# Splitting the mixed tokens at the entry of an MLP: two remainders earlier on VectorE, two on GpSimd

## The chip, the cores and the metric

One core of a Trainium2 chip. The time is the device time of one launch in microseconds, as the median of the runs shown. TensorE (PE in the profile) multiplies matrices, VectorE (DVE) and GpSimd (POOL) do elementwise work, ScalarE (ACT) activations and copies, SyncE (SP) issues DMAs.

## What is computed

A decoder step of two layers on 544 tokens (512 of a prompt, 32 of decoding requests) of width 1024: a token mixer and memory attention, and behind each an MLP of width 4096. The MLP is what matters here:

```python
x = x + jnp.concatenate([mix, mem_out], axis=-1) @ p['w_out'][l]
h2 = rmsnorm(x, p['norm2'][l])
x = x + jnp.square(jax.nn.relu(h2 @ p['w_mlp1'][l])) @ p['w_mlp2'][l]
```

## The kernel before

All data is float32. A product of precision near float32 is made of three passes of TensorE over operands split in two: a high part (a copy in the format that TensorE reads, made by ScalarE) and a remainder (operand less high part, a subtraction of two SBUF operands, made by VectorE or GpSimd). Tokens stand in columns, 544 of them in two halves of 272, features on 128 partitions in eight blocks k; KQ is 4.

The up projection of an MLP has 32 blocks of 128 output features. The first four (PLAIN) are made by `up_plain(j)`: eight blocks k times three passes times two halves, 48 matmuls each. From the fifth on two blocks form a pair, which `up_pair(n)` makes out of seven products q = 0 to 6 in place of eight. The products q = 2, 3 and 6 use mixed tokens: sums and differences of the token halves, three of 272 columns for each kk = 0 to 3, held in `mixed_tokens` (high parts at index 0, remainders at index 1). They come about thus, for each kk: VectorE mixes (`mix_tokens`, L1440: three instructions L1445, L1446, L1447 of 272 columns), ScalarE takes the high part of all three (`mixed_high`, L1063, the instruction L1066, 816 columns, semaphore `tok_hi`), and then VectorE takes the remainder (`mixed_token_rest`, L1449, the instruction L1452, 816 columns, semaphore `tok_lo`). TensorE waits for `tok_lo` only in the product q = 2 of the first pair (n = FIRST_DOWN).

Each engine works off its own list in program order, and the lists are held together by semaphores. Around the entry of an MLP they read so.

VectorE: the output projection's last block k = 7 (`out_units`), in which kk = 0 and 1 have been mixed at k = 5 and 6; `rest(u0 + KT - 1 + HL)`, a weight remainder (L1413, 1024 columns); mixing of kk = 2 and 3; a weight remainder; `inverse(r)` (L1433 and the reciprocal L1434, of 544 columns), which waits for ScalarE's root; a weight remainder; then for j = 0 to 3 `plain(j)`: a ReLU times the inverse root out of PSUM (L1537, semaphore `unit_out`), at j = 1 the four remainders of mixed tokens, and remainders of the first pair's weights (`up_rest`, L1503, 512 columns): q = 0 after j = 1, q = 1 and 2 after j = 2, q = 3 and 4 ahead of the ReLU of j = 3, q = 5 and 6 after it. The ReLU of j = 2 waits for the first hidden remainder of GpSimd, that of j = 3 for the second.

ScalarE: high parts of mixed tokens 1, then a weight's, of 2 and 3, the root (L1044), a weight's; then for each j the square of the ReLU (L1106, L1107) and high parts of the pair's weights (L1089): q = 0 behind j = 0, q = 1 and 2 behind j = 1, q = 3 and 4 behind j = 2, q = 5 and 6 behind j = 3; then the high part of a down weight (L1102) and the copy L1127 of product 0 from PSUM (semaphore `up_copied`), for which TensorE waits ahead of product q = 4.

GpSimd: the sum of squares (L1985); then in turn the hidden remainder of j = 0 (L2023), weight sums L2001 and L2007 (for q = 1 and 2), the hidden remainder of j = 1, the difference L2010 (for q = 3), the hidden remainder of j = 2, the difference L2014 (for q = 5), the hidden remainder of j = 3. ScalarE's high parts of q = 1, 2, 3 and 5 wait for these.

Of the kernel before, what the change touches and what calls it, by code (L numbers as in the profile page):

```python
# [52 lines left out]
KQ = KT // 2  # L53
# [81 lines left out]
def build(nc, xT, memT, hist, params, consts, ropes, weights, memK, memV, cacheK, cacheV, pages,  # L135
          o_y, o_pool, o_memk, o_memv, o_k, o_v, o_pools, o_vs):
    F32, F32R, I32 = mybir.dt.float32, mybir.dt.float32r, mybir.dt.int32
    ALU, ACT, AX = mybir.AluOpType, mybir.ActivationFunctionType, mybir.AxisListType

    ctx = ExitStack()  # L140
    with ctx:
# [13 lines left out]
        def place(name, shape, dt, at):  # L155
            return nc.alloc_sbuf_tensor_at(name, shape, dt, offset=at)
# [48 lines left out]
        mixed_tokens = place("mixed_tokens", [P, 3, 2, KQ, HALF], F32R, kv_at)  # L205
        mixed_raw = place("mixed_tokens_raw", [P, 3, 2, KQ, HALF], F32, kv_at)
# [44 lines left out]
        def sem(name):  # L251
            return ctx.enter_context(nc.semaphore(name))
# [39 lines left out]
        tok_raw, tok_hi, tok_lo = sem("tok_raw"), sem("tok_hi"), sem("tok_lo")  # L292
# [28 lines left out]
        def halves(ap):  # L321

            return ap.rearrange("p (a b) -> p a b", a=2)
# [47 lines left out]
        def hidden_tile(n, c):  # L371

            return 4 * (n // 2 % 2) + 2 * (n % 2) + c
# [1032 lines left out]
        def _(dve):  # L1406
# [33 lines left out]
            def mix_tokens(l, kk):  # L1440

                dve.wait_ge(tok_raw, KT * l + KQ + kk + 1)
                at = Z[:, KQ + kk, :]
                t2, t3, t4 = (mixed_raw[:, c, 1, kk, :] for c in range(3))
                own.chain(dve.tensor_tensor(t3, at[:, HALF:TOK], T[:, kk, HALF:TOK], ALU.subtract))  # L1445
                own.chain(dve.tensor_tensor(t2, t3, T[:, kk, 0:HALF], ALU.add))  # L1446
                dve.tensor_tensor(t4, at[:, 0:HALF], t2, ALU.subtract).then_inc(tok_mixed, 1)  # L1447

            def mixed_token_rest(l, kk):  # L1449

                dve.wait_ge(tok_hi, KQ * l + kk + 1)
                dve.tensor_tensor(mixed_tokens[:, :, 1, kk, :], mixed_raw[:, :, 1, kk, :],  # L1452
                                  mixed_tokens[:, :, 0, kk, :].bitcast(F32), ALU.subtract).then_inc(tok_lo, 1)
# [55 lines left out]
            def mlp(u0, r, g, dst):  # L1509
                l = int(u0 == U_MLP1)  # L1510
# [13 lines left out]
                def add_odd(i, d):  # L1524
                    k = 2 * (d % 4) + 1
                    dve.wait_ge(unit_done, i * 16 + (u0 + down_unit(d) + 1))
                    dve.tensor_tensor(halves(X[:, k, :]), ps[:, 2:4, 0:HALF], halves(X[:, k, :]), ALU.add)\  # L1527
                        .then_inc(unit_out, 1)

                def plain(j):  # L1530
                    if j == PLAIN - 1:
                        for q in range(3, 5):
                            up_rest(u0, 0, FIRST_DOWN, q)
                    dve.wait_ge(unit_done, u0 + j + 1)
                    if j >= 2:
                        dve.wait_ge(hid_lo, DOWNS * l + j - 1)
                    dve.scalar_tensor_tensor(out=halves(T[:, j % 2, :]),  # L1537
                                             in0=ps[:, PLAIN_BANK[j]:PLAIN_BANK[j] + 2, 0:HALF], scalar=0.0,
                                             in1=halves(rms[:, :]), op0=ALU.max, op1=ALU.mult).then_inc(unit_out, 1)
                    if j == 1:  # L1540
                        for kk in range(KQ):
                            mixed_token_rest(l, kk)
                    for q in ((), (0,), (1, 2), (5, 6))[j]:
                        up_rest(u0, 0, FIRST_DOWN, q)

                def step(i, n):
# [50 lines left out]
                    ahead(6)  # L1597
                    add_odd(i, d0 + 1)

                mix_tokens(l, 2)  # L1600
                mix_tokens(l, 3)
                rest(u0 + HL)
# [370 lines left out]
        def _(pool):  # L1973
# [43 lines left out]
            def mlp(u0, hidden, r):  # L2017
                l = int(u0 == U_MLP1)

                def hidden_rest(i, n, c):  # L2020
                    pool.wait_ge(hid_hi, i * 8 + (DOWNS * l + 2 * n + c + 1))
                    k = hidden_tile(n, c)
                    pool.tensor_tensor(hidden[:, 1, k, :], T[:, c, :], hidden[:, 0, k, :].bitcast(F32),  # L2023
                                       ALU.subtract).then_inc(hid_lo, 1)

                def step(i, n):
                    if n < PAIRS - 1:
                        up_weights(u0, i, n + 1, (0, 1, 2))
                    for c in range(2):
                        hidden_rest(i, n, c)  # L2030
                    if n < PAIRS - 1:
                        up_weights(u0, i, n + 1, (3,))

                for j in range(PLAIN):
                    hidden_rest(0, j // 2, j % 2)
                    up_weights(u0, 0, FIRST_DOWN, ((0, 1), (2,), (3,), ())[j])
                with pool.Fori(0, LOOPS) as i:
                    for n in range(2, 6):
                        step(i, n)
                step(0, PAIRS - 2)  # L2040
                step(0, PAIRS - 1)
                sum_squares(r)
# [229 lines left out]
```

## Time and profile before

| what | value |
|---|---|
| median of 3 runs | 1232.44 us (1228.14 to 1232.98) |
| the profiled execution's own time | 1230.28 us |
| its span, first to last instruction | 1228.4 us |
| mean granted clock of TensorE | 0.987 |
| TensorE matmuls busy | 1171.5 us (95%) |
| VectorE busy | 851.2 us (69%) |
| ScalarE busy | 518.3 us (42%) |
| GpSimd busy | 432.8 us (35%) |

Busy times are of one profiled execution. An instruction's duration includes time in which it is held up after its start. Starts of instructions that follow one another on an engine lie about 0.1 us closer than the durations say, since ends and starts overlap.

### The profile page before, as it was taken

The page shows a single profiled execution, that of the slowest core. Times are in us where ns is not written, and L with a number is a line of the kernel's source. Part 1 is how long each engine was busy: PE and PEld are TensorE (multiplying, and loading weights), DVE is VectorE, ACT ScalarE, POOL GpSimd, SP SyncE. Part 2 cuts the span into 40 slices and gives each one's busy share as a digit, 9 for nine tenths or more (in the row PEclk, how much of TensorE's full clock was granted, in tenths as well). Part 3 has the DMA queues.
Part 4 walks back from the last instruction along what each step waited for, and adds up shares of the span by engine and source line. Part 5 has one row for each costly group of instructions (what it writes and reads, how often), then busy time and mean ns, then how long its engine had stood idle before and what let it go on. Part 6 is the DMA issues. An engine that isn't in the chain of part 4 may idle for free.

```text
span 1228.4 us, 23853 instructions
## 1 busy us (share of the span) xinstructions
PE 1171.5 (95%) x9338; PEld 1121.7 (91%) x9338; DVE 851.2 (69%) x1332; ACT 518.3 (42%) x1014; POOL 432.8 (35%) x332
## 2 busy tenths in 40 slices
PE   5999899999999999999999998899899999999996
PEld 5878898999999999999899855699899999999996
DVE  7767679776776776656643777769877767767644
ACT  7545444443343433344422277735443434333321
POOL 3364025453443444321037110022544434444312
PEclk9999999899999999999999999999999999999997
DMA  7632421323223223323254267122232132232212
GB/s 282 226 124 60 143 86 52 137 70 105 102 69 121 86 69 121 124 101 104 89 157 127 78 246 242 57 86 87 70 106 101 69 121 86 69 120 86 79 60 73
DMA packets 46228, 134.95 MB, mean 110 GB/s; under 512 B 4178, under 2 KB 6354, under 8 KB 45490
## 3 DMA queue, kind: packets, MB, share of 16 engines
q1 hardware_dynamic: 45026, 125.39, 30.3%
q0 software_dynamic: 1104, 8.15, 2.2%
q8 instruction: 74, 1.21, 0.4%
q14 instruction: 24, 0.20, 0.1%
HBM read 123.15 MB, written 7.03 MB: 106 GB/s over the span
## 4 chain that ended last, share of the span: by engine, by line
PE 77%; DVE 12%; ACT 4%; POOL 3%; DMA 2%; issue 2%; ACTq 0%; DVEq 0%; SPq 0%; POOLq 0%
PE psum L642 30%; PE psum L624 23%; PE psum L557 17%; DVE weights_split L1413 2%; DVE inv_rms L1434 1%; DVE mixed_tokens L1452 1%; PE psum L809 1%; DMA rotated<-keys 1%; DMA rotated<-projected 1%; POOL projected L2119 1%; POOL projected L2120 1%; ACT weights_split L1024 1%; PE psum L714 1%; PE psum L728 1%; POOL rotated L2118 1%
## 5 line engine op out<-in xcount | busy, mean ns | idle before, releaser
L642 PE MATMUL psum<-operand_b,weights_split 128*128 128x272 f32 x1536 | 195.0, 288 | 0.2 <-DVE residual L1521 0.2
L642 PE MATMUL psum<-operand_a,weights_split 128*128 128x272 f32 (+1 forms) x1536 | 194.8, 288 | 0.0
L642 PEld LDWEIGHTS psum<-operand_b,weights_split 128*128 128x128 f32 x1536 | 193.5, 189 | 0.4 <-issue 0.4
L642 PEld LDWEIGHTS psum<-operand_a,weights_split 128*128 128x128 f32 x1536 | 193.4, 189 | 0.0
L557 PE MATMUL psum<-operand_b,weights_split 128*128 128x272 f32 x1344 | 175.9, 291 | 4.4 <-DVE weights_split L1413 4.2
L557 PEld LDWEIGHTS psum<-operand_b,weights_split 128*128 128x128 f32 x1344 | 171.1, 190 | 9.4 <-DVE weights_split L1413 5.2
L557 PE MATMUL psum<-operand_a,weights_split 128*128 128x272 f32 (+1 forms) x948 | 126.1, 292 | 17.2 <-DVE weights_split L1413 13.3
L557 PEld LDWEIGHTS psum<-operand_a,weights_split 128*128 128x128 f32 x948 | 120.4, 191 | 23.3 <-issue 16.9
L1024 ACT ACTIVATE weights_split<-weights_raw 128x1024 fp32r<-128x1024 f32 (+1 forms) x66 | 66.5, 1008 | 142.1 <-PE psum L557 127.6
L2001 POOL TENSOR_TENSOR mem_keys<-weights_raw 128x512 f32<-128x512 f32 x28 | 39.0, 1393 | 218.8 <-DMA weights_raw<-in_weights 218.8
L1515 DVE TENSOR_TENSOR weights_split<-weights_raw,weights_split 128x1024 fp32r<-128x1024 f32 x64 | 90.5, 1414 | 6.5 <-ACT weights_split L1102 6.5
L1527 DVE TENSOR_TENSOR residual<-psum,residual 128x544 f32<-128x544 f32 x63 | 45.6, 723 | 67.3 <-PE psum L642 67.3
L1413 DVE TENSOR_TENSOR weights_split<-weights_raw,weights_split 128x1024 fp32r<-128x1024 f32 (+1 forms) x66 | 81.1, 1229 | 12.6 <-ACT weights_split L1024 12.5
L624 PE MATMUL psum<-mixed_tokens,up_weights_a 128*128 128x272 f32 x672 | 89.2, 289 | 0.0
L624 PEld LDWEIGHTS psum<-mixed_tokens,up_weights_a 128*128 128x128 f32 x672 | 86.4, 188 | 0.0
L1985 POOL TENSOR_TENSOR squares_sum<-squares_sum,squares 128x544 f32<-128x544 f32 (+1 forms) x35 | 52.3, 1496 | 83.4 <-ACT squares L1036 82.8
L2023 POOL TENSOR_TENSOR operand_a<-staging,operand_a 128x544 fp32r<-128x544 f32 x32 | 53.1, 1676 | 78.5 <-ACT staging L1107 78.4
L2023 POOL TENSOR_TENSOR operand_b<-staging,operand_b 128x544 fp32r<-128x544 f32 x32 | 52.6, 1660 | 78.4 <-ACT staging L1107 78.3
L1503 DVE TENSOR_TENSOR up_weights_a<-weights_raw,up_weights_a 128x512 fp32r<-128x512 f32 x56 | 78.9, 1409 | 1.6 <-ACT up_weights_a L1089 1.3
L1102 ACT ACTIVATE weights_split<-weights_raw 128x1024 fp32r<-128x1024 f32 x64 | 67.1, 1048 | 17.2 <-PE psum L642 17.2
L1521 DVE TENSOR_TENSOR residual<-psum,residual 128x544 f32<-128x544 f32 x64 | 46.0, 718 | 26.7 <-PE psum L642 26.6
L1089 ACT ACTIVATE up_weights_b<-mem_values 128x512 fp32r<-128x512 f32 x28 | 17.7, 631 | 105.3 <-POOL mem_values L2014 105.3
(288 smaller groups left out, 2077.7 us busy)
## 6 DMA issues: line engine op xcount, KB each, us to landing
weights_raw<-in_weights SPq DMA_DIRECT2D x186, 512.0 KB, 3.7
cache_tiles<-in_page_k SPq DMA_DIRECT2D x16, 384.0 KB, 4.1
cache_tiles<-in_page_v SPq DMA_DIRECT2D x16, 384.0 KB, 4.2
cache_tiles<-in_mem_k SPq DMA_DIRECT2D x8, 512.0 KB, 4.7
cache_tiles<-in_mem_v SPq DMA_DIRECT2D x8, 512.0 KB, 5.1
residual<-in_x SPq DMA_DIRECT2D x1, 2176.0 KB, 11.7
rotated<-projected POOLq DMA_DIRECT2D x4, 408.0 KB, 7.1
rotated<-keys POOLq DMA_DIRECT2D x4, 408.0 KB, 7.9
```

Source lines behind the costliest of these rows:

```text
L557: mm = pe.matmul(ps[:, 2 * (j % PS) + hf, 0:n], w(wr), act[:, ar, k, hf * n:(hf + 1) * n], start=(q == 0 and wr == 0 and ar == 0), stop=(q ...
L624: mm = pe.matmul(up_bank(UP_BANK[q]), up_split(q)[:, wr, lo_of(kk)], up_tokens(h2, q, ar, kk), start=(kk == 0 and wr == 0 and ar == 0), st ...
L642: mm = pe.matmul(ps[:, bank, 0:part.stop - part.start], w(wr), hidden[:, ar, 4 * (c % 2) + kk, part], start=(kk == 0 and wr == 0 and ar == 0),
L1024: act.activation(split[:, s % HL, 0, 0:n], raw[:, s, 0:n], ACT.Copy).then_inc(weight_hi, 1)
L1102: act.activation(split[:, d % HL, 0, :], raw[:, u % RAW, :], ACT.Copy).then_inc(weight_hi, 1)
L1413: dve.tensor_tensor(split[:, s % HL, 1, 0:n], raw[:, s, 0:n], split[:, s % HL, 0, 0:n].bitcast(F32), ALU.subtract).then_inc(weight_lo, 1)
L1503: ins = dve.tensor_tensor(at[:, 1, :], up_source(q, u % RAW), at[:, 0, :].bitcast(F32), ALU.subtract)
L1515: dve.tensor_tensor(split[:, d % HL, 1, :], raw[:, u % RAW, :], split[:, d % HL, 0, :].bitcast(F32), ALU.subtract).then_inc(weight_lo, 1)
L1521: dve.tensor_tensor(halves(X[:, k, :]), ps[:, 0:2, 0:HALF], halves(X[:, k, :]), ALU.add)\
L1527: dve.tensor_tensor(halves(X[:, k, :]), ps[:, 2:4, 0:HALF], halves(X[:, k, :]), ALU.add)\
L1985: pool.tensor_tensor(sq_sum[:, 0:cols], a, SQ[:, k % 2, 0:cols], ALU.add).then_inc(sq_summed, 1)
L2023: pool.tensor_tensor(hidden[:, 1, k, :], T[:, c, :], hidden[:, 0, k, :].bitcast(F32), ALU.subtract).then_inc(hid_lo, 1)
```

## The change

The four remainders of mixed tokens leave `plain(1)` of VectorE. Those of kk = 0 and 1 go to VectorE ahead of the mixing of kk = 2 and 3; those of kk = 2 and 3 go to GpSimd, ahead of its first hidden remainder. It holds for both MLPs. TensorE's waits are the same.

```diff
@@ -1537,9 +1537,6 @@
                                              in1=halves(rms[:, :]), op0=ALU.max, op1=ALU.mult).then_inc(unit_out, 1)
-                    if j == 1:
-                        for kk in range(KQ):
-                            mixed_token_rest(l, kk)
                     for q in ((), (0,), (1, 2), (5, 6))[j]:
                         up_rest(u0, 0, FIRST_DOWN, q)
 
@@ -1597,6 +1594,8 @@
+                mixed_token_rest(l, 0)
+                mixed_token_rest(l, 1)
                 mix_tokens(l, 2)
                 mix_tokens(l, 3)
                 rest(u0 + HL)
@@ -2031,6 +2030,10 @@
+                for kk in (2, 3):
+                    pool.wait_ge(tok_hi, KQ * l + kk + 1)
+                    pool.tensor_tensor(mixed_tokens[:, :, 1, kk, :], mixed_raw[:, :, 1, kk, :],
+                                       mixed_tokens[:, :, 0, kk, :].bitcast(F32), ALU.subtract).then_inc(tok_lo, 1)
                 for j in range(PLAIN):
                     hidden_rest(0, j // 2, j % 2)
```

## Rows read from the trace of the kernel before

**Rows 1.** Stages of the span: window, its length, busy time of each engine, clock, DMA

```profile
210.00:222.00 12.00, 9.03 (x52) 8.84 (x51) 9.46 (x13) 5.05 (x8) 3.33 (x3) 0.74 0.38 127
```

**Rows 2.** Waits, 165 to 245 us: engine, line, releaser, us in total, times, longest

```profile
PE psum L624 <- ACT up_partial L1127: 3.0, 1, 3.0
...
PE psum L624 <- DVE staging L1537: 1.2, 1, 1.2
```

**Rows 3.** Timeline of TensorE: start us, duration, instruction, count [idle before, releaser]

```profile
207.04 3.26 PE L624 MATMUL psum<-operand_a,up_weights_a 128*128 128x272 f32 x24 [1.21 <-DVE staging L1537]
...
216.29 5.78 PE L624 MATMUL psum<-operand_a,up_weights_b 128*128 128x272 f32 x24 [2.97 <-ACT up_partial L1127]
...
223.65 12.20 PE L642 MATMUL psum<-operand_b,weights_split 128*128 128x272 f32 x96
```

**Rows 4.** Instructions on mixed_tokens: durations ns min/median/max; whole span, then 197 to 200

```profile
L1452 DVE TENSOR_TENSOR mixed_tokens<-mixed_tokens_raw,mixed_tokens x8: 999/2092/2183, 197.4 to 862.4; 128x816 fp32r<-128x816 f32 x8
...
L1452 DVE TENSOR_TENSOR mixed_tokens<-mixed_tokens_raw,mixed_tokens x2: 1000/1584/2169, 197.4 to 198.3; 128x816 fp32r<-128x816 f32 x2
```

**Rows 5.** Chain that ended last, in order of time: start us, duration, what

```profile
200.39 4.11 DVE mixed_tokens L1452 x2
```

**Rows 6.** Timeline of VectorE, 185 to 213 us

```profile
185.42 0.44 DVE L1445 TENSOR_TENSOR mixed_tokens_raw<-projected,staging 128x272 f32<-128x272 f32 x1
185.89 1.48 DVE L1446 TENSOR_TENSOR mixed_tokens_raw<-mixed_tokens_raw,staging 128x272 f32<-128x272 f32 x1
...
189.07 1.22 DVE L1413 TENSOR_TENSOR weights_split<-weights_raw,weights_split 128x1024 fp32r<-128x1024 f32 x1
190.80 0.73 DVE L1433 TENSOR_TENSOR inv_rms<-rms_up,inv_rms 128x544 f32<-128x544 f32 x1 [0.51 <-ACT rms_up L1044]
191.56 3.55 DVE L1434 RECIPROCAL inv_rms<-inv_rms 128x544 f32<-128x544 f32 x1
...
196.11 1.35 DVE L1537 SCALAR_TENSOR_TENSOR staging<-psum,inv_rms 128x544 f32<-128x544 f32 x2
197.38 7.12 DVE L1452 TENSOR_TENSOR mixed_tokens<-mixed_tokens_raw,mixed_tokens 128x816 fp32r<-128x816 f32 x4
...
206.19 0.71 DVE L1537 SCALAR_TENSOR_TENSOR staging<-psum,inv_rms 128x544 f32<-128x544 f32 x1
...
211.93 0.71 DVE L1537 SCALAR_TENSOR_TENSOR staging<-psum,inv_rms 128x544 f32<-128x544 f32 x1
```

**Rows 7.** Timeline of GpSimd, 184 to 223 us

```profile
184.66 2.42 POOL L1985 TENSOR_TENSOR squares_sum<-squares_sum,squares 128x544 f32<-128x544 f32 x1 [5.36 <-ACT squares L1036]
198.15 1.45 POOL L2023 TENSOR_TENSOR operand_b<-staging,operand_b 128x544 fp32r<-128x544 f32 x1 [11.07 <-ACT staging L1107]
199.56 2.05 POOL L2001 TENSOR_TENSOR mem_keys<-weights_raw 128x512 f32<-128x512 f32 x1
201.75 1.87 POOL L2007 TENSOR_TENSOR mem_values<-mem_keys,weights_raw 128x512 f32<-128x512 f32 x1
203.59 2.12 POOL L2023 TENSOR_TENSOR operand_b<-staging,operand_b 128x544 fp32r<-128x544 f32 x1
205.67 1.72 POOL L2010 TENSOR_TENSOR weights_raw<-weights_raw 128x512 f32<-128x512 f32 x1
...
213.96 1.33 POOL L2023 TENSOR_TENSOR operand_b<-staging,operand_b 128x544 fp32r<-128x544 f32 x1 [2.50 <-ACT staging L1107]
221.47 1.28 POOL L2001 TENSOR_TENSOR mem_keys<-weights_raw 128x512 f32<-128x512 f32 x1 [6.18 <-DMA weights_raw<-in_weights]
```

**Rows 8.** Timeline of ScalarE, 184 to 217 us

```profile
184.48 0.87 ACT L1066 ACTIVATE mixed_tokens<-mixed_tokens_raw 128x816 fp32r<-128x816 f32 x1
...
189.19 0.89 ACT L1066 ACTIVATE mixed_tokens<-mixed_tokens_raw 128x816 fp32r<-128x816 f32 x1 [0.41 <-DVE mixed_tokens_raw L1447]
190.05 0.72 ACT L1044 ACTIVATE rms_up<-psum,tiny 128x544 f32<-128x544 f32 x1
...
215.78 0.37 ACT L1127 ACTIVATE up_partial<-psum 128x272 f32<-128x272 f32 x1
```

**Rows 9.** Groups of GpSimd instructions by shape: count, busy us, mean ns, idle before

```profile
L2094 POOL TENSOR_TENSOR window_partial<-pool_line 128x679 f32<-128x679 f32 x3 | 4.0, 1318 | 11.3 <-ACT pool_line L1278 11.3
```

## Prediction

> **What bounds the kernel now.** I began with the page: TensorE is busy 95% of the 1228.4 us span, so away from its few gaps nothing on another engine counts. The table of stages around the entry of the first MLP puts the gaps in one place: between 210 and 222 us TensorE is busy for 9.03 of 12 us, at a granted clock of 0.74 [rows 1]. The waits of that stretch name two: 1.2 us for a ReLU of VectorE (DVE staging L1537) and 3.0 us for a copy of ScalarE (ACT up_partial L1127) [rows 2]. TensorE's own timeline shows where. After the four plain units it stands still until 207.04, runs the first four products of the pair, and stops again until 216.29; the 24 matmuls after that take 5.78 us, where the same number took 3.26 us before, which is the lower of the two clock levels (1.2 against 2.4 GHz) after some 3 us of standing still [rows 3]. From 223.65 it runs on without a gap. So one moment matters in this entry: the end of L1127 at 216.15. Whatever moves it moves all that follows, to the end of the kernel. The second entry is the same 660 us later: L1452 runs first at 197.4 and last at 862.4 [rows 4].
>
> The chain that ended last leads back from there through VectorE's four mixed-token remainders, L1452, from 197.38 to 204.42, the block that the change takes away [rows 5, 6]. Read by that alone, 7 us leave the path. I look next at why the block takes 7.04 us. One such instruction takes 1.00 us when alone; the median is 2.09 [rows 4]. Beside VectorE's rows stand GpSimd's [rows 6, 7]. GpSimd starts a hidden remainder (L2023) at 198.15 and ends at 199.60; a weight sum (L2001) ends at 201.61, another (L2007) at 203.62. VectorE's remainders end at 0.8 to 0.9 us after each of these. And GpSimd's own operations, 1.28 us for 512 columns and 1.33 for 544 when nothing stands beside them, take 1.87 to 2.12 there, because each waits in turn for one of VectorE's [rows 7]. The two engines take turns, whole instruction by whole instruction, when both read two SBUF operands. The ReLU L1537, which reads PSUM, isn't held up: 0.71 us at 206.19 beside GpSimd's L2010 [rows 6, 7]. The reciprocal L1434 has no GpSimd operation beside it: GpSimd idles from 187.1 to 198.15 [rows 7].
>
> The Trainium skill's page "SBUF — State Buffer" (section "Who interferes with whom") says this too: a VectorE instruction with two SBUF inputs and a GpSimd instruction that reads SBUF share one port pair, and the second to issue fully blocks. By that rule the change only moves blocking from one place to another, and the trace agrees, with 2.09 us for an instruction of 1.00. The same section says that an operation with at most one SBUF input isn't blocked, which would leave the reciprocal free; no row here shows it.
>
> **Part 1: remainders 0 and 1 ahead of mixing 2 and 3.** Their inputs are long ready (ScalarE's second high part ends at 185.35 [rows 8]). VectorE reaches the place at 185.42. Two instructions at a pitch of 0.91 (197.38 to 198.29) are 1.82 us. The sum of squares on GpSimd (L1985, 184.66 for 2.42) cost mixing 2 about 1.05 us, seen as 1.48 instead of 0.44 at L1446 [rows 6, 7]; it now costs the remainders the same or 0.15 more. So all behind it comes 2.0 us later: the third weight remainder at 191.05 for 189.07. The root waits for both on ScalarE (the last high part at 189.19, then 0.72 for the root L1044 at 190.05), so L1433 goes from 190.80 to 192.8, and with it the reciprocal, the fourth weight remainder and the first ReLU at 196.11 [rows 6, 8]. That is 2.0 us on the path, and there is no idle stretch of VectorE left to take it up: it idles 0.51 us ahead of L1433, for the root, and the root is late by the same 2.0.
>
> **Part 2: remainders 2 and 3 on GpSimd.** One of 816 columns: the trace has none. From above, by columns from the 512 in 1.28 [rows 7], 2.04 us; from below, by the 679 in 1.32 of L2094 [rows 9], 1.58. Taken: 1.95, since the rows of this stage with equal operands (1.28 for 512, 1.33 for 544) are the nearer kind. The Trainium skill's "GPSIMD Engine Reference" (section "Elementwise — side-by-side cycle accounting") puts a two-input operation at 1.96 times VectorE's time; from VectorE's 1.00 us here that would be an estimate of 1.96, and would change nothing in the sum.
>
> GpSimd idles from 187.1 to 198.15 [rows 7], so its own time is free. The place isn't: mixing 2 would end at 189.83, ScalarE's high part of it (0.87) at 190.74, and GpSimd ask at 190.82 (it follows ScalarE by 0.08, as 198.15 shows), while VectorE is in its last mixing step. Next on VectorE come L1413 (third weight remainder) and L1433, both with two SBUF operands. Who gets the turn when GpSimd has been waiting? Mostly GpSimd: its ends less its own durations give starts at 200.33, 202.34 and 204.38, each time ahead of a VectorE instruction that follows at once [rows 7], and so in nearly all places of the trace where the two meet. One kind is the other way: at 185.42 a short VectorE instruction behind L1413 got in first (0.44 us, not held up), with GpSimd waiting since 184.66 [rows 6, 7].
> By the usual turn, remainder 2 runs 191.05 to 193.0; L1413 then to 194.03 (1.03 behind the release); remainder 3, ready since 192.1, from 194.0 to 195.95; L1433 behind it, and the reciprocal starts 0.65 later, at 196.6 for 191.56. That is 5.04 late: 2.0 of part 1 and 3.0 of part 2. TensorE's third and fourth units wait for the weight remainders for some 0.6 and 1.0 us; this is nothing by itself, for TensorE waits again for L1127 in any case.
>
> **Part 3: what leaving the old place gives.** I replay the turns from the first ReLU (s), each GpSimd operation at 1.28 or 1.36, each 512-column remainder L1503 at 0.57 behind a release. GpSimd's hidden remainder starts at s+2.05 (198.15 less 196.11), ends 3.41; L1503 for q=0 to 3.95; sum L2001 to 5.23, sum L2007 from 5.33 to 6.61; L1503 for q=1 to 7.15; second hidden remainder to 8.51; L1503 for q=2 to 9.05; difference L2010 to 10.33. Before, L2010 ended at 207.39, which is s+11.28 [rows 7]. ScalarE's high part for q=3 needs L2010 (before, it also stood behind the late third ReLU): it is at 10.38 to 11.00. VectorE's remainder 3 waits out the third hidden remainder to 12.23, remainder 4 waits out L2014 to 14.05, the fourth ReLU is at 13.97, before s+15.82 (211.93) [rows 6]. From there to the end of L1127 nothing changes: 216.15 less 211.93 is 4.22, together s+18.19 against s+20.04. So the 7.04 us block is worth only 1.85 us: GpSimd's five operations and three of VectorE's between them are a chain of 8.3 us of their own, which was hidden under the block. The third ReLU does come early (s+3.93), so TensorE's gap of 1.21 us goes; its products 0 to 3 end sooner, and it waits the longer for L1127.
>
> **The sum.** Per entry: +5.04 − 1.85 = +3.2 us for L1127, and TensorE with it. The clock: TensorE stands still for more than 3 us, as before, and restarts at the lower level for about the same time; I count no difference. Two entries: +6.4 us. Against the profiled execution's 1230.28 us (1228.4 of span and 1.9 around it) that is 1236.7. This execution lies 2.2 under the median of the runs, 1232.44; on the median it is 1238.8, my forecast. With 1.58 or 2.04 us for a GpSimd remainder, twice per entry, L1127 is +2.45 or +3.37 late: 1237.3 or 1239.2 on the median.
>
> **Rivals.**
> (a) One collision, not two: either L1433 gets in ahead of remainder 3, as L1445 did behind an L1413 at 185.42, or L1413 gets in ahead of remainder 2. The other remainder then runs under the reciprocal of 3.5 us, which reads one SBUF operand, as the ReLU does. The first ReLU is 3.26 late, L1127 by +1.4, two entries +2.8: 1235.2 on the median. For it: L1445 gets in at both entries [rows 6, 7]. Against: everywhere else GpSimd is first.
> (b) No cost from part 2 at all: 2.0 − 1.85, +0.15 per entry, 1232.7. It asks that GpSimd's 816-column form doesn't take the turns; nothing in the trace is like that.
> (c) The naive reading, and the other side: the chain behind the ReLUs shrinks by the whole block less the delay, 7.04 − 2.0 = 5.0 us, enough to close both gaps (1.21 and 2.97) and with them the half-clock stretch (36 matmuls in 7.4 us where 4.6 would do [rows 3], of which VectorE's sums, due one after the other, would still take 0.7). That is −6.3 per entry, 1219.8. It needs L2010 to end before 203; it decides where GpSimd's five operations (6.6 us without any wait, from s+2.05) stop being the later ones, and they alone are already at s+8.7. Any gain at all needs the first ReLU less than 1.85 late, and part 1 alone is 2.0.
> (d) Worse: VectorE also loses the turn for L1447, the last step of mixing 3, to remainder 2, so that ScalarE's high part, remainder 3 and the root are late as well, by up to 1.95 less the 1.1 that L1413 would not be late again; with both later collisions it adds some 1.5 us per entry: 1242.
>
> **Chances.** Forecast (two collisions) 0.5, (a) 0.29, (b) 0.08, (c) 0.04, (d) 0.09. What the measurement can tell from no change is about 0.5%, 6.2 us. The forecast's +6.4 lies at this bound, and with the bounds of the GpSimd duration about six parts in ten of it are above: slower 0.5 × 0.6 + 0.09 = 0.39; faster 0.04; the rest, 0.57, within. The range takes in (a) and the lower half of (b), and some of (d), with the scatter of the runs: 1231.5 to 1242.
>
> **What would show it.** In the profile after: the two L1452 of VectorE ahead of L1445 at 185.4, and L1433 at about 194.0 instead of 190.80, itself near 2.6 us long; an L1413 of about 3 us near 191; the new GpSimd line twice at about 2 us alone and more with waiting; the first L1537 near 201.1; L2010 ending about 10.3 us behind it; L1127 near 219.3. TensorE's gap ahead of the pair's products gone, a longer one ahead of its fifth product, still followed by the lower clock. If L1433 starts at 192.8 with 0.73 us, (b) holds; if L1434 starts near 194.8, (a). I am wrong in kind if L1127 comes before 216.

## The result and the profile after

The changed kernel takes 1234.74 us in the median of 16 runs, the kernel before 1229.04 in 16 runs beside it: a ratio of 1.0042, 95% interval [1.0031, 1.0053], which is 5.2 us (3.8 to 6.5). The two profiled executions differ by 4.6 us of span (1233.0 against 1228.4), but only 3.1 of that lies in the two entries; 1.7 is a stretch between them in which TensorE's clock differed (last part of the experiments). It is a small loss, of the sign and kind that were forecast, and somewhat less than the 6.4 us of the sum. The kernel before itself came out 3.4 us lower with more runs (1229.04 for 1232.44); the forecast time of 1238.8 stood on that median, and this is most of what it is too high by. The time alone would fit rival (a) better (1235.2); the difference to the kernel before, at least 3.8 us, doesn't fit its 2.8, and the profiles below show two collisions and not one.

What follows compares times from one marker: the start of the weight remainder L1413 ahead of the place where remainders 0 and 1 now stand, 184.28 in the kernel before and 184.52 in the changed one. (In the expectations below it is called the second weight remainder.)

VectorE in the entry of the first MLP, the changed kernel (start, duration, instruction), against [rows 6]:

```profile
184.52 1.22 DVE L1413 TENSOR_TENSOR weights_split<-weights_raw,weights_split 128x1024 fp32r<-128x1024 f32 x1
185.66 1.92 DVE L1452 TENSOR_TENSOR mixed_tokens<-mixed_tokens_raw,mixed_tokens 128x816 fp32r<-128x816 f32 x2
...
187.96 1.50 DVE L1446 TENSOR_TENSOR mixed_tokens_raw<-mixed_tokens_raw,staging 128x272 f32<-128x272 f32 x1
...
191.15 2.97 DVE L1413 TENSOR_TENSOR weights_split<-weights_raw,weights_split 128x1024 fp32r<-128x1024 f32 x1
194.05 2.47 DVE L1433 TENSOR_TENSOR inv_rms<-rms_up,inv_rms 128x544 f32<-128x544 f32 x1
196.55 3.55 DVE L1434 RECIPROCAL inv_rms<-inv_rms 128x544 f32<-128x544 f32 x1
...
201.10 1.34 DVE L1537 SCALAR_TENSOR_TENSOR staging<-psum,inv_rms 128x544 f32<-128x544 f32 x2
...
204.95 0.71 DVE L1537 SCALAR_TENSOR_TENSOR staging<-psum,inv_rms 128x544 f32<-128x544 f32 x1
...
214.57 0.71 DVE L1537 SCALAR_TENSOR_TENSOR staging<-psum,inv_rms 128x544 f32<-128x544 f32 x1
```

The two remainders aren't held up (1.92 us for both), mixing 2 is held up at L1446 as before, and the third weight remainder takes 2.97 us in place of 1.22, L1433 2.47 in place of 0.73. GpSimd beside it, against [rows 7] (L1984, L2000, L2006, L2009 and L2022 here are L1985, L2001, L2007, L2010 and L2023 of before, L2035 is new):

```profile
184.89 4.27 POOL L1984 TENSOR_TENSOR squares_sum<-squares_sum,squares 128x544 f32<-128x544 f32 x1 [5.36 <-ACT squares L1036]
190.93 5.01 POOL L2035 TENSOR_TENSOR mixed_tokens<-mixed_tokens_raw,mixed_tokens 128x816 fp32r<-128x816 f32 x2 [1.77 <-ACT mixed_tokens L1066]
203.12 1.35 POOL L2022 TENSOR_TENSOR operand_b<-staging,operand_b 128x544 fp32r<-128x544 f32 x1 [7.19 <-ACT staging L1107]
204.43 1.73 POOL L2000 TENSOR_TENSOR mem_keys<-weights_raw 128x512 f32<-128x512 f32 x1
206.30 1.30 POOL L2006 TENSOR_TENSOR mem_values<-mem_keys,weights_raw 128x512 f32<-128x512 f32 x1
207.56 1.82 POOL L2022 TENSOR_TENSOR operand_b<-staging,operand_b 128x544 fp32r<-128x544 f32 x1
209.35 1.72 POOL L2009 TENSOR_TENSOR weights_raw<-weights_raw 128x512 f32<-128x512 f32 x1
```

L2035 asks at 190.93 and runs ahead of L1413; the second of them gets its turn behind L1413 and ahead of L1433. From 203.12 the five operations follow one another until 211.07, with no idle time of more than 0.14 us between them.

TensorE and ScalarE's copy, against [rows 3] and [rows 8]:

```profile
202.58 4.08 PE L684 MATMUL psum<-operand_a,weights_split 128*128 128x272 f32 x19 [2.10 <-DVE staging L1537]
...
210.15 3.19 PE L624 MATMUL psum<-operand_a,up_weights_a 128*128 128x272 f32 x24
...
218.93 4.77 PE L624 MATMUL psum<-operand_a,up_weights_b 128*128 128x272 f32 x24 [2.57 <-ACT up_partial L1127]
...
225.06 6.16 PE L642 MATMUL psum<-operand_b,weights_split 128*128 128x272 f32 x48
```

```profile
218.41 0.38 ACT L1127 ACTIVATE up_partial<-psum 128x272 f32<-128x272 f32 x1
```

TensorE no longer waits ahead of the pair's first product (210.15 has no idle time before it), but ahead of the fourth plain unit, 2.10 us, for the second ReLU. It waits for L1127 again: 2.57 us here, 4.1 in the other five entries that were profiled of this kernel. In this one the 19 matmuls at 202.58 take 4.08 us, the lower clock level, so that TensorE comes to the wait later; the end of L1127 isn't moved by that (34.26 us behind the marker in this entry, 34.29 to 34.35 in the others). By these rows it ends 34.27 us behind the marker, where it was 31.87: 2.40 us later.

The waits of TensorE in the stretch from 184 to 230 us (releaser, us in total, times, longest), against [rows 2]:

```profile
PE psum L624 <- ACT up_partial L1127: 2.6, 1, 2.6
PE psum L684 <- DVE staging L1537: 2.1, 1, 2.1
```

### The profile page after: what moved, and what is told of

Same layout as the page of the kernel before. It is cut to its first block, busy times and chain, and to the rows that moved or that the text cites. A ratio compares the mean times of both kernels' runs of the same rounds, so it can differ in the third digit from the quotient of the medians.

```text
span 1233.0 us, 23853 instructions
## 1 busy us (share of the span) xinstructions
PE 1175.0 (95%) x9338; PEld 1124.9 (91%) x9338; DVE 848.3 (69%) x1328; ACT 518.7 (42%) x1014; POOL 442.5 (36%) x336
## 4 chain that ended last, share of the span: by engine, by line
PE 76%; DVE 11%; POOL 4%; ACT 3%; DMA 3%; issue 2%; SPq 0%; ACTq 0%; DVEq 0%; POOLq 0%
PE psum L642 29%; PE psum L624 23%; PE psum L557 17%; DVE weights_split L1413 2%; PE psum L809 1%; DMA rotated<-projected 1%; POOL rotated L2121 1%; POOL projected L2123 1%; DMA rotated<-keys 1%; ACT weights_split L1024 1%; PE psum L714 1%; POOL projected L2122 1%; PE psum L728 1%; DVE inv_rms L1434 1%; PE psum L791 1%
## 5 line engine op out<-in xcount | busy, mean ns | idle before, releaser
L2000 POOL TENSOR_TENSOR mem_keys<-weights_raw 128x512 f32<-128x512 f32 x28 | 37.4, 1334 | 219.0 <-DMA weights_raw<-in_weights 212.7
L1413 DVE TENSOR_TENSOR weights_split<-weights_raw,weights_split 128x1024 fp32r<-128x1024 f32 (+1 forms) x66 | 84.7, 1284 | 12.6 <-ACT weights_split L1024 12.5
L1984 POOL TENSOR_TENSOR squares_sum<-squares_sum,squares 128x544 f32<-128x544 f32 (+1 forms) x35 | 56.0, 1601 | 83.4 <-ACT squares L1036 82.8
L2022 POOL TENSOR_TENSOR operand_a<-staging,operand_a 128x544 fp32r<-128x544 f32 x32 | 52.4, 1654 | 73.9 <-ACT staging L1107 73.8
L2022 POOL TENSOR_TENSOR operand_b<-staging,operand_b 128x544 fp32r<-128x544 f32 x32 | 52.4, 1655 | 73.8 <-ACT staging L1107 73.8
L1521 DVE TENSOR_TENSOR residual<-psum,residual 128x544 f32<-128x544 f32 x64 | 46.0, 718 | 28.1 <-PE psum L642 28.1
```

What stands on the lines that cost most here:

```text
L1413: dve.tensor_tensor(split[:, s % HL, 1, 0:n], raw[:, s, 0:n], split[:, s % HL, 0, 0:n].bitcast(F32), ALU.subtract).then_inc(weight_lo, 1)
L1521: dve.tensor_tensor(halves(X[:, k, :]), ps[:, 0:2, 0:HALF], halves(X[:, k, :]), ALU.add)\
L1984: pool.tensor_tensor(sq_sum[:, 0:cols], a, SQ[:, k % 2, 0:cols], ALU.add).then_inc(sq_summed, 1)
```

## Experiments

Each profile gives the same two distances for each entry: from the marker to the end of L1127 (or its copy on another line), and to TensorE's first matmul of the down blocks, from which it runs on with at most one short wait (0.6 us or less, for VectorE's L1521).

Medians of different rows come from different sets of runs, so the ratio, made against runs of the kernel before on the same chip, is the figure to compare.

| kernel | median us | ratio to before, 95% interval | marker to end of L1127, entries 1, 2 | marker to down blocks |
|---|---|---|---|---|
| before | 1229.0 | | 31.87, 31.85 | 39.37, 38.55 |
| before, 2nd profile | | | 31.88, 31.88 | 38.01, 38.52 |
| before, 3rd profile | | | 31.86, 31.84 | 38.14, 37.67 |
| changed | 1234.7 | 1.0042 [1.0031, 1.0053] | 34.26, 34.30 | 40.54, 40.47 |
| changed, 2nd profile | | | 34.30, 34.35 | 40.55, 40.61 |
| changed, 3rd profile | | | 34.29, 34.29 | 40.56, 41.73 |
| e1, VectorE's part alone | 1229.9 | 1.0007 [0.9994, 1.0019] | 31.94, 31.95 | 38.22, 38.89 |
| e2, GpSimd's part alone | 1232.1 | 1.0025 [1.0010, 1.0040] | 33.10, 33.09 | 40.37, 39.35 |
| e3, changed, GpSimd behind the root | 1228.8 | 1.0000 [0.9987, 1.0012] | 31.44, 31.45 | 37.70, 37.71 |
| e4, sums first | 1225.2 | 0.9969 [0.9955, 0.9983] | 29.88, 29.87 | 35.70, 36.15 |
| e5, sums first, remainders spread | 1218.9 | 0.9923 [0.9903, 0.9943] | 26.22, 26.22 | 33.37, 33.35 |
| e6, as e5, one remainder on GpSimd | 1219.3 | 0.9903 [0.9883, 0.9924] | 26.68, 26.72 | 32.92, 32.95 |

### One part alone: e1 and e2

The theory is that of the prediction: two engines that take turns over whole instructions, so that GpSimd's new work costs VectorE its full length on the path to the first ReLU, and GpSimd's own chain behind the ReLUs limits what the removed block gives. The rival is that part 1's two instructions are the whole loss.

e1 against the kernel before:

```diff
                     if j == 1:
-                        for kk in range(KQ):
+                        for kk in (2, 3):
                             mixed_token_rest(l, kk)
...
+                mixed_token_rest(l, 0)
+                mixed_token_rest(l, 1)
                 mix_tokens(l, 2)
```

> Of the change only part 1: remainders 0 and 1 on VectorE ahead of mixing 2 and 3; remainders 2 and 3 stay on VectorE behind the second ReLU, nothing new on GpSimd. Theory (turns of two engines, GpSimd's chain of five): the first ReLU is 1.8 to 2.0 us later than before (near 198.0 in the first entry), the two remainders left behind the ReLUs cost about 0.8 us of GpSimd's chain, so the ReLU to the end of L1127 takes 18.4 us and L1127 ends near 216.5, +0.3; two entries 0 to +2 us. Rival 1 (the whole loss is part 1's two instructions on the path): +2.4 us for L1127 and some +5 us in all, as with the whole change. Rival 2 (the naive reading: half of the 7 us block has gone): L1127 1.5 us earlier, -3 us in all.

e2 against the kernel before:

```diff
                     if j == 1:
-                        for kk in range(KQ):
+                        for kk in (0, 1):
                             mixed_token_rest(l, kk)
...
+                for kk in (2, 3):
+                    pool.wait_ge(tok_hi, KQ * l + kk + 1)
+                    pool.tensor_tensor(mixed_tokens[:, :, 1, kk, :], mixed_raw[:, :, 1, kk, :],
+                                       mixed_tokens[:, :, 0, kk, :].bitcast(F32), ALU.subtract).then_inc(tok_lo, 1)
                 for j in range(PLAIN):
                     hidden_rest(0, j // 2, j % 2)
```

> Of the change only part 2: remainders 2 and 3 on GpSimd ahead of its first hidden remainder; 0 and 1 stay on VectorE behind the second ReLU. Theory: GpSimd's first remainder takes the turn ahead of the third weight remainder L1413 (near 3 us long instead of 1.22), the second ahead of L1433 (near 2.5 instead of 0.73); the first ReLU 2.8 us late, near 199.0; the ReLU to L1127 18.4 us; L1127 near 217.4, +1.3, two entries +1 to +3 us. Rival 1 (part 1 is the whole loss, GpSimd's part is hidden): the first ReLU within 0.3 us of before and L1127 1.5 us earlier, -3 us in all.

VectorE in e1, then in e2:

```profile
185.07 1.22 DVE L1413 TENSOR_TENSOR weights_split<-weights_raw,weights_split 128x1024 fp32r<-128x1024 f32 x1
...
191.70 1.22 DVE L1413 TENSOR_TENSOR weights_split<-weights_raw,weights_split 128x1024 fp32r<-128x1024 f32 x1
193.33 0.73 DVE L1433 TENSOR_TENSOR inv_rms<-rms_up,inv_rms 128x544 f32<-128x544 f32 x1 [0.42 <-ACT rms_up L1044]
194.09 3.55 DVE L1434 RECIPROCAL inv_rms<-inv_rms 128x544 f32<-128x544 f32 x1
...
198.64 1.35 DVE L1537 SCALAR_TENSOR_TENSOR staging<-psum,inv_rms 128x544 f32<-128x544 f32 x2
199.90 3.09 DVE L1452 TENSOR_TENSOR mixed_tokens<-mixed_tokens_raw,mixed_tokens 128x816 fp32r<-128x816 f32 x2
```

```profile
184.87 1.22 DVE L1413 TENSOR_TENSOR weights_split<-weights_raw,weights_split 128x1024 fp32r<-128x1024 f32 x1
...
189.66 2.96 DVE L1413 TENSOR_TENSOR weights_split<-weights_raw,weights_split 128x1024 fp32r<-128x1024 f32 x1
192.54 2.46 DVE L1433 TENSOR_TENSOR inv_rms<-rms_up,inv_rms 128x544 f32<-128x544 f32 x1
195.04 3.55 DVE L1434 RECIPROCAL inv_rms<-inv_rms 128x544 f32<-128x544 f32 x1
...
199.59 1.34 DVE L1537 SCALAR_TENSOR_TENSOR staging<-psum,inv_rms 128x544 f32<-128x544 f32 x2
200.85 3.10 DVE L1452 TENSOR_TENSOR mixed_tokens<-mixed_tokens_raw,mixed_tokens 128x816 fp32r<-128x816 f32 x2
```

In e1 the first ReLU is at 13.57 us behind the marker for 11.83 before: 1.74 later; L1413 and L1433 keep their 1.22 and 0.73. From it to the end of L1127 it is 18.37 us for 20.04: 1.67 shorter. Together +0.08, and the time is the same within its interval. Part 1 costs on one side what it gives on the other, and in sum nothing, which refutes the first rival (+2.4 us) and the second, the naive reading (1.5 us earlier). In e2 the two collisions are there in full (2.96 and 2.46), the first ReLU is 2.89 later, the rest 18.38; together +1.22, and the ratio agrees (1.0025 is 3.1 us, 1.2 to 4.9; twice 1.22 is 2.4). The two instructions are held up by 1.74 and 1.73 us, 3.47 in all; the 0.51 us that VectorE idled ahead of L1433 before are gone, which takes up most of what is between 3.47 and 2.89. So the GpSimd part makes the loss. The parts don't add to 2.40: 0.08 + 1.22 is 1.30. The delays nearly add (1.74 + 2.89 = 4.63 against 4.75 with both), the gains don't: either two remainders out of the block give 1.67 us, all four only 2.35 (20.04 less 17.69), for then GpSimd's chain is the later one, as e4 tests below.

### The collisions taken away, the work left: e3

e3 against the changed kernel:

```diff
+                pool.wait_ge(root_ready, (R_MLP1 if l else R_MLP0) + 1)
                 for kk in (2, 3):
                     pool.wait_ge(tok_hi, KQ * l + kk + 1)
```

> The whole change, and GpSimd waits for the root (root_ready) before its two remainders, so that they run under the reciprocal. Theory: L1413 and L1433 of VectorE are back at 1.22 and 0.73 us, the reciprocal keeps its 3.55 us with a GpSimd operation beside it (one SBUF operand), the fourth weight remainder waits some 0.3 us for the second GpSimd remainder; the first ReLU comes 2.3 us earlier than with the change and 2.3 later than before; L1127 at 216.1 to 216.5, level with before; in all -3 to -5 us against the change, 0 to +2 against the kernel before. Rival 1 (part 1 is the whole loss): no difference to the change, +5 us. Rival 3 (the reciprocal takes turns too): the reciprocal 5.5 us long, no gain.

VectorE and GpSimd in e3:

```profile
191.69 1.22 DVE L1413 TENSOR_TENSOR weights_split<-weights_raw,weights_split 128x1024 fp32r<-128x1024 f32 x1
193.33 0.73 DVE L1433 TENSOR_TENSOR inv_rms<-rms_up,inv_rms 128x544 f32<-128x544 f32 x1 [0.42 <-ACT rms_up L1044]
194.09 3.55 DVE L1434 RECIPROCAL inv_rms<-inv_rms 128x544 f32<-128x544 f32 x1
197.56 1.30 DVE L1413 TENSOR_TENSOR weights_split<-weights_raw,weights_split 128x1024 fp32r<-128x1024 f32 x1
198.78 1.34 DVE L1537 SCALAR_TENSOR_TENSOR staging<-psum,inv_rms 128x544 f32<-128x544 f32 x2
```

```profile
193.37 4.41 POOL L2036 TENSOR_TENSOR mixed_tokens<-mixed_tokens_raw,mixed_tokens 128x816 fp32r<-128x816 f32 x2 [3.68 <-ACT rms_up L1044]
200.81 1.37 POOL L2022 TENSOR_TENSOR operand_b<-staging,operand_b 128x544 fp32r<-128x544 f32 x1 [3.03 <-ACT staging L1107]
```

The two remainders run from 193.37 to 197.78, and the reciprocal takes its 3.55 us beside them. L1413 and L1433 are back at 1.22 and 0.73 us; only the fourth weight remainder is held up, by 0.14. L1127 is 2.84 us earlier than with the change (31.44 for 34.28), 0.42 earlier than before, and the time is that of the kernel before: 1.0000 [0.9987, 1.0012]. One wait on GpSimd, with the same work on the same engines, takes the whole loss back. So the loss is where GpSimd's two operations fall, not that they are on GpSimd. It also shows that the change has next to nothing to give even where GpSimd's part costs VectorE only 0.14 us: 7 us of VectorE's block are gone, and L1127 gains 0.42.

### GpSimd's chain: e4, e5 and e6

If GpSimd's five operations behind the ReLUs are what the block was hiding, then moving three of them away must help even with the block where it was. The three need only the loaded weights. e4 against the kernel before:

```diff
+                pool.wait_ge(root_ready, (R_MLP1 if l else R_MLP0) + 1)
+                up_weights(u0, 0, FIRST_DOWN, (0, 1, 2))
                 for j in range(PLAIN):
                     hidden_rest(0, j // 2, j % 2)
-                    up_weights(u0, 0, FIRST_DOWN, ((0, 1), (2,), (3,), ())[j])
+                    up_weights(u0, 0, FIRST_DOWN, ((), (), (3,), ())[j])
```

> The kernel before, with its four remainders on VectorE behind the second ReLU, and one edit on GpSimd: it waits for the root and then makes the weight sums L2001, L2007 and the difference L2010 of the first pair ahead of its first hidden remainder, under the reciprocal. Theory (GpSimd's chain of five is what the block was hidden behind or hid): the first ReLU 0.5 us later than before, the VectorE block 6.3 us or so with only two hidden remainders between, L1127 near 214.5, 1.7 us earlier than before, TensorE's gap of 1.2 us ahead of the pair gone; two entries -3 to -5 us. Rival (GpSimd's chain isn't on the path and the block of VectorE alone is): L1127 as before or later by 0.5, 0 to +1 us in all.

GpSimd and VectorE in e4:

```profile
191.63 1.83 POOL L2001 TENSOR_TENSOR mem_keys<-weights_raw 128x512 f32<-128x512 f32 x1 [3.77 <-ACT rms_up L1044]
193.61 1.29 POOL L2007 TENSOR_TENSOR mem_values<-mem_keys,weights_raw 128x512 f32<-128x512 f32 x1
194.98 1.30 POOL L2010 TENSOR_TENSOR weights_raw<-weights_raw 128x512 f32<-128x512 f32 x1
199.31 1.46 POOL L2023 TENSOR_TENSOR operand_b<-staging,operand_b 128x544 fp32r<-128x544 f32 x1 [3.04 <-ACT staging L1107]
200.93 1.93 POOL L2023 TENSOR_TENSOR operand_b<-staging,operand_b 128x544 fp32r<-128x544 f32 x1 [0.15 <-ACT staging L1107]
```

```profile
197.28 1.34 DVE L1537 SCALAR_TENSOR_TENSOR staging<-psum,inv_rms 128x544 f32<-128x544 f32 x2
198.55 6.09 DVE L1452 TENSOR_TENSOR mixed_tokens<-mixed_tokens_raw,mixed_tokens 128x816 fp32r<-128x816 f32 x4
```

The sums run under the reciprocal, the block takes 6.01 us (198.55 to 204.56) for 7.04, and L1127 is 1.99 us earlier than before in both entries; the time is 0.9969 [0.9955, 0.9983], 3.8 us less. The rival expected none.

e5 adds to this what the change was after, in another way: VectorE's remainders go where VectorE has nothing else to do. e5 against e4:

```diff
-                    if j == 1:
-                        for kk in range(KQ):
-                            mixed_token_rest(l, kk)
+                    for kk in ((), (0,), (), (1, 2, 3))[j]:
+                        mixed_token_rest(l, kk)
                     for q in ((), (0,), (1, 2), (5, 6))[j]:
```

> As the run with the sums first (GpSimd makes L2001, L2007 and L2010 of the first pair under the reciprocal, before its first hidden remainder), and the four remainders of mixed tokens stay on VectorE but no longer in one block: number 0 behind the second ReLU, where VectorE would wait for ScalarE in any case, 1 to 3 behind the fourth ReLU, still ahead of TensorE's product q=2. Theory (nothing of the entry stands behind GpSimd's chain or a block of VectorE any more; the fourth ReLU comes as soon as TensorE has made the fourth plain unit): L1127 ends some 27 us behind the start of the second weight remainder (before 31.9, sums first 29.9), ahead of the moment at which TensorE needs it; both gaps of TensorE close or are under 0.5 us, its clock stays at the upper level, and the down blocks start some 33 us behind that remainder (before 39.4 and 38.6). Two entries: -10 to -12 us, 1217 to 1219. Rival (another wait takes its place: VectorE's own sums L1561 to L1575 or ScalarE's order hold TensorE in the pair): L1127 early but a new gap inside the pair, -5 to -7 us in all.

TensorE's timeline in e5, and its waits from 184 to 230 us:

```profile
210.91 2.15 PE L624 MATMUL psum<-mixed_tokens,up_weights_a 128*128 128x272 f32 x15 [0.98 <-DVE mixed_tokens L1452]
212.90 3.18 PE L624 MATMUL psum<-operand_a,up_weights_b 128*128 128x272 f32 x24
...
217.59 6.16 PE L642 MATMUL psum<-operand_b,weights_split 128*128 128x272 f32 x48
```

```profile
PE psum L624 <- DVE mixed_tokens L1452: 1.0, 1, 1.0
...
PE psum L642 <- DVE residual L1521: 0.4, 1, 0.4
```

L1127 ends 26.22 us behind the marker, ahead of TensorE's need; the 24 matmuls at 212.90 take 3.18 us for 5.78 [rows 3] (4.0 to 5.8, waits between them included, in the six profiled entries of the kernel before), the upper clock level; TensorE never stands still for more than 1.0 us in this stretch. The time is 1218.86 us, 0.9923 [0.9903, 0.9943], 9.5 us less than before, a little short of the 10 to 12 expected: the last remainder comes 1.0 us late for product q = 2, where under 0.5 was expected.

e6 takes that wait away (remainder 0 on GpSimd behind the sums, 1 behind the second ReLU, 2 and 3 behind the fourth). e6 against e5:

```diff
-                    for kk in ((), (0,), (), (1, 2, 3))[j]:
+                    for kk in ((), (1,), (), (2, 3))[j]:
...
                 up_weights(u0, 0, FIRST_DOWN, (0, 1, 2))
+                pool.wait_ge(tok_hi, KQ * l + 1)
+                pool.tensor_tensor(mixed_tokens[:, :, 1, 0, :], mixed_raw[:, :, 1, 0, :],
+                                   mixed_tokens[:, :, 0, 0, :].bitcast(F32), ALU.subtract).then_inc(tok_lo, 1)
```

> The spread version (sums first under the reciprocal, remainders in VectorE's idle places), and remainder 0 on GpSimd behind the three sums, where VectorE has only ReLUs out of PSUM; remainder 1 behind the second ReLU, 2 and 3 behind the fourth on VectorE. In the spread version TensorE still waits 1.0 us in product q=2 for the last remainder, since three of them and a hidden remainder of GpSimd take 3.9 us behind the fourth ReLU. Theory: that wait goes, the first hidden remainder of GpSimd comes up to 0.5 us later, the fourth ReLU up to 0.7 later; the down blocks start 32.3 to 32.8 us behind the second weight remainder (33.4 in the spread version); -1 to -2 us against it, 1217 or so. Rival (GpSimd's chain again): the fourth ReLU and the last remainders are late by as much as GpSimd's remainder takes, 0 to +2 us against the spread version.

The wait in q = 2 is gone; 0.4 us for VectorE's L1562 stand in its place (the wait for L1521 behind it is 0.6 us for 0.4), and the down blocks start 0.4 us sooner in both entries, less than the 0.6 to 1.1 expected. The ratio 0.9903 [0.9883, 0.9924] overlaps that of e5: which is faster was not settled. Both beat the kernel before and the changed one.

### What differs from execution to execution

The profiles of before and after differ by more than the entries in one place that no edit touches. It had to be seen whether that belongs to the change.

> The kernel before, once more with a profile, to see what differs from one execution to the next. Theory: the entry of each MLP repeats to 0.1 us on VectorE, ScalarE and GpSimd (31.9 us from the second weight remainder to the end of L1127), while TensorE's clock in the 36 matmuls behind it and in the attention between 780 and 790 us varies: 5.7 to 7.4 us for the matmuls, and 3 to 4 us at the attention. Rival: both stretches repeat as well, and are set by the kernel.

> The changed kernel, once more with a profile. Theory: 34.3 us from the second weight remainder to the end of L1127 in both entries again; the slow stretch of TensorE in the attention between 780 and 792 us, which the first profile of the changed kernel had and that of the kernel before had not, may be there or not, so it is no part of the change. Rival: it is there again, and half of what the two profiles differ by belongs to it.

> The kernel before, a third profile. From the first down block of the first MLP to the second MLP's weight remainder, code that the change doesn't touch, the first two took 620.7 and 619.0 us. Theory A (the clock of TensorE in the attention near 780 us differs from execution to execution, whatever the kernel): 619 to 622.5, as in any kernel here. Theory B (the change's later entry brings the slow stretch about): 619 to 621, no stretch at half clock longer than 5 us.

> The changed kernel, a third profile. The same stretch took 622.4 and 621.8 us in its first two, with 8 us at half clock between 781 and 791. Theory A (execution to execution): 619 to 622.5, the slow stretch there or not. Theory B (brought about by the change): there again, 621.5 or more.

A stage of the attention in layer 1, from the table of stages (window, length, busy time of each engine, clock, DMA), in the changed kernel's first profile, then in its third:

```profile
785.00:790.00 5.00, 4.67 (x20) 4.41 (x20) 0.54 (x2) 2.59 (x13) 0.59 (x2) 0.50 0.01 3
```

```profile
785.00:790.00 5.00, 4.57 (x36) 4.29 (x36) 3.69 (x13) 4.14 (x15) 0.29 (x1) 1.00 0.00 0
```

And in e6, which isn't the changed kernel and reaches this stage earlier:

```profile
780.00:785.00 5.00, 5.00 (x24) 4.71 (x24) 1.96 (x9) 2.38 (x9) 0.29 (x1) 0.50 0.00 0
```

The slow stretch is there in the first two profiles of the changed kernel and missing in the third; it is there in e3 and in e6, and missing in all three of the kernel before and in e1, e2, e4 and e5. From the first down block to the second entry's marker the kernel before took 620.7, 619.0 and 619.5 us, the changed one 622.4, 621.8 and 619.1, e1 to e6 619.1, 620.3, 621.5, 621.2, 619.7 and 623.1. These times go with how long the trace shows the clock at the lower level on the way: 619.0 to 619.7 in the four executions with some 3 us of it, 619.5 to 621.2 in the four with 7, 621.5 to 623.1 in the four with 10 to 14. So theory A holds as far as it goes: some 3 to 4 us of scatter, with TensorE's clock, and not peculiar to the changed kernel. What starts a long slow stretch wasn't found, and three profiles each can't exclude that the change makes it more frequent; the timed difference, 5.2 us with an interval of 1.3 to either side, leaves it little room beside the 4.8 of the two entries.

## Why the prediction was right

**The bound.** That L1127 decides the entry holds in every kernel up to e4: its shift and that of the down blocks go together (changed, in the mean of six entries: 34.30 for 31.86, +2.43, and 40.74 for 38.38, +2.37). In e5 and e6 it is early enough to decide nothing.

**Part 1.** Forecast 2.0 us on the path; e1 shows 1.74. The two remainders put off the mixing by 1.83 us (2.97 behind the marker for 1.14), the mixing pays for the sum of squares what it paid before (L1446 at 1.49 for 1.48), and VectorE's idle time ahead of L1433 shrinks from 0.51 to 0.42.

**Part 2.** Both collisions happened where and as they were placed: L1413 2.97 us long at 6.63 behind the marker (forecast about 3 at 6.8), L1433 2.47 (forecast 2.6) at 9.53 (forecast 9.8), the reciprocal 12.03 behind (forecast 12.3). The duration that the trace of before couldn't show was taken at 1.95; undisturbed in e3 the shortest is 1.952. The usual turn held, with GpSimd ahead of both; rival (a), the one collision, did not occur in any profile, and rival (b) would have needed what e3 had to force by a wait. The rows that spoke for (a) repeated, though, and more so: see the last section.

**Part 3.** This is the mis-sized term. The replay gave 18.19 us from the first ReLU to the end of L1127, measured 17.69; the gain of the removed block is 2.35, not 1.85. The mechanism and the order of the turns were right (GpSimd's chain nearly without a free moment, L2009 ending 9.97 us behind the ReLU for a forecast of 10.33, the fourth ReLU at 13.47 for 13.97). What was too long is the step from the end of a remainder of VectorE to the end of GpSimd's operation behind it, set at GpSimd's whole own 1.28 or 1.36 us: it took 1.14, 1.23, 1.14 and 1.16 us, 0.12 to 0.14 less each, and four such turns stand ahead of the fourth ReLU, which makes the 0.50. The rows of before had it already: 1.13 to 1.22 us from the end of VectorE's instruction to the end of GpSimd's behind it, as from 206.27 to 207.39 at L2010 [rows 6, 7].

**TensorE's third and fourth units.** The prediction had them wait 0.6 us and 1.0 us for the weight remainders. The third doesn't wait; the fourth waits 2.10 for the second ReLU, whose PSUM banks the unit writes (PLAIN_BANK gives 2 for j = 1 and j = 3). The step was missed, since in the kernel before the ReLU had been ready long ahead. It changed nothing in the end, as was said of the whole waiting there: TensorE stands still for L1127 in any case.

**The clock.** Counted at no difference. In the mean of six entries L1127 and the down blocks shift by the same (2.43 and 2.37), so this holds; one entry alone varies by 1.7 us (37.67 to 39.37 in the kernel before). The longer wait that was forecast ahead of the fifth product came in five entries of six (4.1 us for 3.0), and the lower level behind it in each.

**The sum.** 2 × (4.75 − 2.35) = 4.8 us; timed, 5.2 [3.8, 6.5]; forecast 6.4, from 2 × (5.04 − 1.85). Both terms erred the same way, by 0.3 and 0.5 us per entry. The measured 0.42% is below the 0.5% named as what can be told, which with 16 runs on a side was too cautious.

**Rival (c), the naive reading** by the chain that ended last, was wrong by a sign: the block stood on that chain, and its removal gave 2.35 of 7.04 us. What it hoped for, both gaps of TensorE closed and the upper clock level, is what e5 reaches but for one gap of 1.0 us, by moving GpSimd's work too, 5.0 us per entry at the down blocks (33.36 for 38.38), less than the 6.3 of its estimate.

The Trainium skill's page "SBUF — State Buffer" (section "Who interferes with whom") says that of two contending instructions the second to issue blocks until the first ends. The L1433 of 2.47 us here agrees with it. The sum of squares of 4.27 us, which three later instructions of VectorE passed (last section), doesn't follow from it, and there the measurement decides. That an operation with one SBUF input isn't blocked, as the same section has it, e3 shows for the reciprocal, 3.55 us beside L2036; the rows of before showed it for the ReLU alone [rows 6, 7].

## What to carry to other kernels

A block that stands on the chain that ended last is worth no more than its distance to the next chain beside it; replay the other engine's work from the same start, with its turns, before you count the block's length. Where VectorE and GpSimd both read two SBUF operands, an idle GpSimd is not free: an operation of 1.95 us held VectorE up by 1.75 here, as VectorE had something of this kind to do right then, so place it under something of VectorE's with one such operand, as a reciprocal or a ReLU out of PSUM, if need be by a wait on a semaphore that marks the place. And put first those operations of a slow helper that need nothing late.

## What the runs showed of the hardware

Who gets the turn is not only a matter of who waited longer. In the changed kernel GpSimd's sum of squares asks at 184.89, during L1413, and VectorE's next three instructions go first (two L1452 of 816 columns and one L1445, at full pace), so that the sum takes 4.27 us and ends at 189.16; in every profiled entry of the changed kernel, e1 and e3 it is the same to 0.01 us (4.26 or 4.27). Right after, at 190.93, GpSimd asks during L1447 and goes ahead of L1413, in all the entries that have it there. In the kernel before L1445 went ahead once in the same place [rows 6, 7]. What decides it wasn't tried. It repeated in every profile of a kernel, so the trace of a kernel was a good guide here for the turns that it shows, and less so for new ones.
